# GpSimd's split of the weight blocks: a cast in place of a multiplication by ones, and the loop written out

## The reference

```python
def conv_ffn(xn, w_in, conv_w, conv_b, w_out, rows):
    a, v = _split(xn @ w_in, (D_FF, D_FF))          # D_FF = 2816
    if rows is None:
        a = dwconv_seq(a, conv_w[1])                # context: three taps
    else:
        a = dwconv_grid(a, conv_w, rows)            # latent: nine taps
    h = jax.nn.gelu(a + conv_b) * v
    return h @ w_out
```

## Time and profile before

| | |
|---|---|
| runs | 3961.45, 3971.77, 3974.27 us; median 3971.77 |
| span of the profiled execution | 3966.6 us |
| busy, TensorE matmuls / weight loads | 3448.7 / 3332.8 us |
| busy, VectorE | 1854.5 us |
| busy, GpSimd | 968.1 us |
| of it roundings (L693), 206 | 420.2 us |
| of it subtractions (L695), 206 | 542.8 us |

### The profile page before, as it was taken

How to read it: one execution, slowest core, us unless ns; L and a number is a source line. 1 busy time by engine, 2 the same in 40 slices (tenths; PEclk the granted TensorE clock), 3 DMA queues, 4 the chain that set the end, 5 groups by cost and what they waited for, 6 DMA issues and landing times. The chain is left out here.

```text
span 3966.6 us, 49337 instructions
## 1 busy us (share of the span) xinstructions
PE 3448.7 (87%) x19579; PEld 3332.8 (84%) x19579; DVE 1854.5 (47%) x2483; ACT 736.0 (19%) x1381; POOL 968.1 (24%) x435
## 2 busy tenths in 40 slices
PE   8899999969799999999978889886868888888885
PEld 8788899959799999999977778776868888888885
DVE  2333332230755554555554244253365566655555
ACT  1333321121300010000004233232120000000000
POOL 1111122203123333333221212111212333233330
PEclk8898999979899999999988899898989999999997
DMA  3111121132211111111131010112310010110102
GB/s 155 39 52 51 51 74 51 61 101 73 86 54 57 59 69 58 63 53 53 53 105 56 27 42 24 38 36 79 112 39 32 32 37 33 36 37 32 37 32 96
DMA packets 86088, 225.58 MB, mean 57 GB/s; under 512 B 8000, under 2 KB 45120, under 8 KB 85872
## 3 DMA queue, kind: packets, MB, share of 16 engines
q1 hardware_dynamic: 44064, 163.16, 11.9%
q10 hardware_dynamic: 41936, 61.17, 4.5%
HBM read 193.89 MB, written 30.41 MB: 57 GB/s over the span
## 5 line engine op out<-in xcount | busy, mean ns | idle before, releaser
L712 PE MATMUL bank<-xh,wh 128*128 128x384 f32 x3888 | 1378.2, 354 | 225.3 <-DVE cc L2116 141.7
L712 PE MATMUL bank<-xl,wh 128*128 128x384 f32 x3888 | 1350.3, 347 | 0.0
L712 PE MATMUL bank<-xh,wl 128*128 128x384 f32 x3888 | 1346.1, 346 | 0.0
L693 POOL TENSOR_TENSOR wh<-raw,ones 128x1024 fp32r<-128x1024 f32 x206 | 420.2, 2040 | 2893.2 <-PE bank L712 1831.6
L712 PEld LDWEIGHTS bank<-xh,wh 128*128 128x128 f32 x3888 | 771.6, 198 | 258.5 <-DVE cc L2116 124.4
L712 PEld LDWEIGHTS bank<-xl,wh 128*128 128x128 f32 x3888 | 770.9, 198 | 0.5
L712 PEld LDWEIGHTS bank<-xh,wl 128*128 128x128 f32 x3888 | 768.7, 198 | 0.0
L2108 DVE SCALAR_TENSOR_TENSOR cc<-pad,cw,cc 128x1024 f32<-128x1024 f32 x352 | 573.8, 1630 | 6.9
L695 POOL TENSOR_TENSOR wl<-raw,wh 128x1024 fp32r<-128x1024 f32 x206 | 542.8, 2635 | 16.2
L712 PE MATMUL bank<-hh,wh 128*128 128x384 f32 x1056 | 373.0, 353 | 69.8 <-DVE y L2138 32.2
L2138 DVE TENSOR_TENSOR y<-y,bank 128x384 f32<-128x384 f32 x480 | 247.1, 551 | 278.1 <-PE bank L712 256.3
(11 more groups left out here) (231 smaller groups left out, 2622.2 us busy)
## 6 DMA issues: line engine op xcount, KB each, us to landing
raw<-in_w SPq DMA_DIRECT2D x206, 512.0 KB, 3.3
ada_w<-in_ada SPq DMA_DIRECT2D x80, 512.0 KB, 3.4
residual_scratch<-y ACTq DMA_DIRECT2D x9, 1536.0 KB, 5.9
xg<-residual_scratch ACTq DMA_DIRECT2D x9, 1536.0 KB, 7.9
xr<-mixer_scratch ACTq DMA_DIRECT2D x16, 576.0 KB, 3.8
front<-in_ada SPq DMA_DIRECT2D x16, 512.0 KB, 8.1
y<-in_x SPq DMA_DIRECT2D x1, 4608.0 KB, 19.6
mixer_scratch<-hout ACTq DMA_DIRECT2D x24, 192.0 KB, 1.9
```

The lines of the kernel that those rows point to most:

```text
L693: nc.gpsimd.tensor_tensor(wh[s][:, :], raw[s][:, :], ones[:, 0:1].broadcast_to([128, 1024]), ALU.mult).then_inc(w_hi[s], 1)
L712: return nc.tensor.matmul(out, lhsT, rhs, start=start, stop=stop)
```

## The change

The rounding at L693 becomes a `tensor_copy` of `raw` into `wh`: one input, one output, and the conversion to fp32r on the way. And the loop over blocks is written out, so that the counts that semaphores are compared with are constants; the table of semaphore steps for a loop (`PER`) loses its row for it. Lines after the table move by one.

```diff
- 'pool.split': {'raw_loaded0': 16, 'raw_loaded1': 16, 'w_hi0': 1, 'w_hi1': 1, 'w_used0': 1, 'w_used1': 1},
...
                 pool.wait_ge(w_used[s], made.before(w_used[s]))
                 made.next(w_used[s])
-                nc.gpsimd.tensor_tensor(wh[s][:, :], raw[s][:, :], ones[:, 0:1].broadcast_to([128, 1024]), ALU.mult).then_inc(w_hi[s], 1)
+                nc.gpsimd.tensor_copy(wh[s][:, :], raw[s][:, :]).then_inc(w_hi[s], 1)
                 pool.wait_ge(w_hi[s], made.next(w_hi[s]))
                 nc.gpsimd.tensor_tensor(wl[s][:, :], raw[s][:, :], wh[s][:, :].bitcast(f32), ALU.subtract).then_inc(w_ready[s], 1)
 
             split(0)
             split(1)
-            with made.loop(pool, "pool.split", NBLK // 2 - 1):
-                for s in range(2):
-                    split(s)
+            for n in range(2, NBLK):
+                split(n % 2)
```

## The result

The changed kernel takes 3900.1 us in the median of four runs (3898.9 to 3904.7), the kernel before 3970.6 beside it: a ratio of 0.9825, with a 95% interval from 0.9811 to 0.9839. That is 70 us faster; the forecast was 3928, its range 3897 to 3960. The span of the profiled execution went from 3966.6 to 3898.2 us.

The account below looks back on a forecast made before the run. GpSimd's rounding instructions hold VectorE off, and TensorE waits for VectorE in the feed-forward stages. Gains of 32 us (second layer), 8 (first) and 4 (first pairs) sum to 44, giving 3928 us, range 3897 to 3960.

Parts of the forecast that it names:

- What bounds the kernel: Feed-forward stages: TensorE waits for VectorE, which GpSimd's rounding instructions hold off; GpSimd's throughput is not the limit.
- The cast's price: GpSimd's cast of a 128x1024 tile was taken at 1.0 us, saving 0.89 us for each meeting with VectorE.
- The second feed-forward part: Second layer's ten pairs of feature tiles: 1.78 us in the convolution plus 1.4 in the down projection, 32 us together.
- The two meetings in the convolution: Second layer, second tile's convolution: two taps that meet the rounding each end 0.89 us earlier, 1.78 us a pair.
- the down projection: Second layer, where VectorE adds products to `y` with taps in between: 1.4 us gained a pair.
- The replay of the taps: Second layer's down projection replayed with the cast: the next tap finds the subtraction running, waits, and ends 1.4 us earlier.
- The first feed-forward part: First layer's ten pairs: the multiplication meets one convolution tap, 0.89 us, taken as 0.8 a pair, 8 us together.
- the 4 for first pairs: First pair of each layer, without a down projection: some five meetings of 0.89 us in the convolutions, 4 us.
- put at nothing as a toss: First layer's down projection: 0.5 us worse if the subtraction precedes the tap, 0.5 to 0.8 better otherwise; counted as nothing.
- the first rival: The subtraction gets ahead of VectorE's tap, which waits up to 2.4 us: 21 us gained in all, 3951 us; chance 0.14.
- the signs named for being wrong: Cast of 1.6 us or more, 3.3 us taps meeting the subtraction, pairs as long at a lower clock, or waits for `wl`.
- Outside the feed-forward parts: VectorE's meetings there are few and covered by TensorE's own matmuls: nothing gained.

Follow-up runs that it names:

- e3: The changed kernel with each cast done twice: 3985.7 us, ratio 1.0036 against the kernel before.
- e2: The changed kernel with a MEMSET of 808 columns, which reads nothing, ahead of each cast: 3946.0 us, ratio 0.9931 against the kernel before.
- e1: The kernel before with the loop over blocks written out and the multiplication kept: 3973.1 us, ratio 1.0002.
- e5: Loop written out, the cast only in the 74 blocks outside the feed-forward parts, the multiplication in the others: 3946.6 us, ratio 0.9947 against the kernel before.
- e7: The changed kernel with 12 further matmuls in the block ahead of the first GLA head: 3910.1 us, ratio 0.9856 against the kernel before.
- e9: The kernel before, loop written out, the cast only in three blocks whose split ends just before a GLA head's store: 3956.4 us, ratio 0.9969.
- e4: Loop written out, the cast only in the 132 blocks of the feed-forward parts, the multiplication in the others: 3931.5 us, ratio 0.9900 against the kernel before.
- e8: The changed kernel with the subtraction in two instructions of 512 columns: 3878.2 us, ratio 0.9770 against the kernel before.
- the quarters: The changed kernel with the subtraction in four instructions of 256 columns: 3854.3 us, ratio 0.9716 against the kernel before.

## Why the prediction was right, and where not

**What bounds the kernel:** right for the feed-forward parts. TensorE waits there for VectorE, and VectorE is held by GpSimd's instructions. In e3 a second cast costs more than the whole gain, and in e2, where only the instructions that read are shorter, all of the first part's gain stays and a third of the second's. TensorE's wait for L2116 fell by 26 us, where 20 to 30 was said.

**The cast's price:** 1.0 us taken, 1.036 measured at best. The nearest row, MEMSET, was the right one; AFFINE_SELECT's 1.64 was far off. The Trainium skill's figure (GPSIMD Engine Reference, section 3.1), by which I estimated 0.88 us, is below it by 0.16.

**The second feed-forward part:** 32 us predicted for the ten pairs, 25.4 measured with the first pair in it. The two meetings in the convolution gave 1.65 us a pair where 1.78 was said. The term that was mis-sized is the down projection, with 1.4 us: from the first addition to `y` to the last it takes 28.5 us instead of 29.0, so 0.5 came. The replay of the taps was right to 0.1 us (a tap of 3.31 replayed, 3.40 measured), and at that tap's end VectorE is 1.2 us ahead, counted from the first addition. But the clock was not in it: the stretch below, which holds this down projection after the change, has a granted clock of 0.94, while the one in the earlier trace rows had 1.00.

```profile
3119.00:3149.00 30.00, 28.14 (x152) 27.82 (x151) 25.50 (x34) 0.58 (x2) 7.48 (x4) 0.94 0.10 35
```

VectorE's single stop of 2.1 us makes TensorE pause for 1.86 us in one piece, where it had paused for 1.53 and 0.94 before (the first two lines), and the clock falls once, for 3.4 us:

```profile
3185.91 0.44 PE L712 MATMUL bank<-hh,wh 128*128 128x384 f32 x1 [1.53 <-DVE y L2138]
3189.23 0.44 PE L712 MATMUL bank<-hh,wh 128*128 128x384 f32 x1 [0.94 <-DVE y L2138]
```

```profile
3139.08 0.44 PE L712 MATMUL bank<-hh,wh 128*128 128x384 f32 x1 [1.86 <-DVE y L2138]
```

At the end of the stretch VectorE waits for TensorE, 0.20 and 0.50 us before the last two additions, where it had not waited before. From one release of TensorE by L2116 to the next the pairs went from 91.0 to 88.6 us in the mean of nine, 2.4 us instead of 3.2.

**The first feed-forward part:** 8 us for ten pairs and some of the 4 for first pairs, 6.7 measured. TensorE's pause became 0.85 us shorter in each pair, here in the kernel before and after:

```profile
1303.59 0.69 PE L712 MATMUL bank<-xh,wh 128*128 128x384 f32 x1 [2.70 <-DVE cc L2116]
```

```profile
1290.63 0.69 PE L712 MATMUL bank<-xh,wh 128*128 128x384 f32 x1 [1.85 <-DVE cc L2116]
```

The down projection, put at nothing as a toss, became slower: in nine of the ten pairs the subtraction goes ahead of the tap, which then takes 3.5 us, and the additions to `y` last 26.95 us instead of 26.32; in the tenth the tap is first (issued at 1233.82, the subtraction at 1234.13), and they last 25.77. From release to release a pair gained 0.6 us, where 0.8 was taken. So the first rival's race was lost in both parts. Its tap of 3.4 us in the down projection was also one of the signs named for being wrong; it cost 0.6 us a pair in the first part, and in the second it is a part of the 0.9 us that the down projection fell short.

**The written-out loop:** nothing predicted, nothing measured (e1).

**Outside the feed-forward parts:** nothing predicted, 36 us measured. This step failed: the term was put at nothing because TensorE's matmuls were to cover VectorE's meetings there and the supply of weights was to be far ahead. I had dismissed the 7.5 us of waits for `wl` by their sum. Three of the four, 5.7 us, lie in the retention heads, and in the kernel before the clock fell at each of them; with the waits about 1 us shorter the stage took 8.8 us less (6 in e5 and e7). And I had followed GpSimd's instruction to TensorE and VectorE but not to the third one it releases: SyncE, which sends the next 512 KB as soon as a subtraction is done, and so sets what the store of a head's outputs meets (e9, 18 us). The 6.7 us of the projections ahead of the GLA heads don't follow the cast in their own blocks (e4, e5, e8) and go with the clock; the remaining 3 us, in the small stages, were not looked into.

So the total lay within its range, with the sign and one of its mechanisms, and the sum of 44 us was short of the span's 68 by 24: 36 us too little from outside the feed-forward parts, 12 us too much from these. That the time fell inside the range was in part luck: its lower end, 3897, had been worked out from a cheaper cast and won races in the feed-forward parts, and neither came; the measured 3900 was reached through stages that the sum had at nothing.

## What to carry to other kernels

An instruction of an engine with much idle time can still be costly by what it holds off: look for instructions of the same shape with different durations on the other engine, and ask which of them is on the path. Follow a shortened instruction to everyone it releases, the DMA queues too; a transfer that starts a microsecond earlier can leave the way free for another. If the held engine has work that doesn't need the shared access, cut the holding instruction into parts: the quarters are three more lines here and gained 46 us, more than half of what the cast did. Look then at what waits for the last part: here that was a transfer, and 10 of the GLA heads' 18 us went again.

## What was not expected of the hardware

- A store of 192 KB lands 1.85 us after its issue alone, 2.4 us with a 512 KB weight transfer issued 1.46 us ahead of it, and 3.7 to 3.9 us with one 0.6 us ahead. Each time it lands 0.5 to 0.7 us after the weights, though it comes from another engine's queue.
- Time that is saved in a wait can count several times: 1.3 to 1.6 us a head in the GLA stage became about 6, as the time at the low clock in it fell from 79 to 44 us (granted clock 0.91 to 0.95 over the stage). And 2.1 us more work cost 7 us elsewhere (e7).
- A MEMSET of GpSimd runs its 773 ns beside VectorE's two-input taps (e2), while a cast of 1036 ns waits for one and takes up to 1.98 us. The longest cast of the changed kernel, 4.40 us, met no tap: started at 986.35 us, it stood while ten two-input instructions on `y` ran, eight of which started later than itself, each before the one ahead had ended. Between two taps there is a gap of 0.03 us or more.
